# Each of the first nine expert matrices fetched when its own place is free; memory keys turned between value groups; one memory-key tile out of the stretch ahead of the experts

## The chip, the core and the metric

The kernel runs on one core of one Trainium2 chip, as one launch. The metric is device time in microseconds. The engines named below are TensorE (PE, with its weight loads PEld), VectorE (DVE), ScalarE (ACT), GpSimd (POOL) and SyncE (SP), which here only starts transfers. All transfers, whoever starts them, run on the core's 16 DMA engines.

## The reference, cut to what matters

One inference step of two layers over 288 tokens of width 1024 (a prompt of 256, and 8 samples of 4), all in float32. Layer 0 mixes tokens by block-sparse attention and a convolution, layer 1 by a chunked spatial gate; then each layer does this:

```python
for l in range(DEPTH):                       # DEPTH = 2
    ...                                      # mixer; out projection; layer norm 3l
    mk, mv = mem_kv(mem_prompt, w_xkv[l])    # 256 memory rows x 2048 columns: keys, values
    mk_p.append(mk); mv_p.append(mv)         # both are outputs too
    xp = layer_norm(ALPHA * xp + cross_attn(xp, mk, mv, w_xq[l], w_xo[l]), ln_g[l, 1], ln_b[l, 1])
    xs = layer_norm(ALPHA * xs + cross_attn(xs, cache_mem_k[l], cache_mem_v[l], w_xq[l], w_xo[l]), ...)
    xp = layer_norm(ALPHA * xp + moe(xp, w_router, router_bias, w_exp_gate[l], w_exp_up[l], w_exp_down[l]), ...)
    xs = layer_norm(ALPHA * xs + moe(xs, ...), ...)
```

`moe` gives each token to 2 of 16 experts. An expert has three float32 matrices of 2 MB each (gate, up, down), so a layer's experts are 48 matrices, 101 MB.

## The kernel before, in words

**Features lie on partitions** in `feats` (`xT`, `zT`, `mixT`, `qT`, each 128 x 8 x 288). Everything that PE sums in the dense stages goes to four PSUM banks `acc` in turn; `tile_order()` (L144) lists every such tile in order with the engine that empties it, and a tile waits for the one four places ahead of it. PE, DVE and ACT run programs written by hand, in order, joined by semaphores.

**Weights** pass through `ring`, six slots of 2 MB. `unit_order()` (L104) is the list of what is loaded into them; unit u goes to slot u % 6 once the unit six places ahead of it has been read (`slot_free`, L576; `READER` names the tile whose sum ends the reading). SP walks this list strictly in order (`load`, L604), so one unit that isn't free yet holds all behind it. `("xkv", l, n)` is a quarter of layer l's memory projection: n = 0, 1 are the key columns, 2, 3 the value columns. PE makes four key tiles `mk` (`memory_keys`, L910; 2 tiles per unit, 16 matmuls of 256 columns each) and four value tiles `mv` (`memory_values`, L926; 8 matmuls of 512 columns each). Layer 1's memory projection doesn't depend on its tokens, so its tiles are spread as filler: `mk` 0 behind the variance of layer 0's second norm, `mk` 1 behind the `xtok` transposes (L1138) and ahead of the `rank` tile (L1147 and below), `mk` 2, 3 and `mv` 0, 1 behind layer 0's last expert, `mv` 2, 3 around layer 1's `vvar`.

**The experts** run as 16 steps in three sets of three matrices (`place`, L560). Sets 0 and 1 are the six ring slots, set 2 is `EXTRA`: two 16 KB-per-partition pieces of `arena` and one of `feats` (over `mixT` and `qT`). The first three steps are experts 0, 1, 2 whatever the routing, so that their nine matrices can be fetched early (L665 to L671). Steps 3 to 15 are in an order that DVE works out from the router (`steps_ready`); step n's three matrices are fetched when step n-3 is done (`expert_used`). A step is one or more chunks of up to 32 tokens: `gate_and_up` (psS), `pick`, `turn_h`, `down` (psV). POOL stores each chunk's rows to `by_slot`, gathers them behind the last step, and the layer's norm follows.

**Cross attention** (`cross`, L948): `values(0)` and `values(1)` (L1001) sum the cached value rows for two groups of four samples; then `mixT` is projected by `xo`, `mean_tile` and `var` tiles make the norm. The key rows of the prompt's memory are turned back (`mktok`, four tiles of four transposes, L1066) to be stored with the value rows by POOL (`out_mem`), between the mean and the variance of this norm.

The only order that matters around the change is the one written out: PE's program, SP's program and the two lists.

Of the kernel before, what the change touches and what calls it, by code (L numbers as in the profile page):

```python
# [14 lines left out]
P = 128  # L15
# [5 lines left out]
DEPTH = 2  # L21
# [82 lines left out]
def unit_order():  # L104
# [5 lines left out]
    for l in range(DEPTH):  # L110
        if l:
            u += [("in_odd", n) for n in range(4)]
# [15 lines left out]
def tile_order():  # L128
# [49 lines left out]
    for l in range(DEPTH):  # L178
        if l:
            add("u", 8, "s")  # L180
            add("vv", 8, "s")
            add("vmean", 1, "v")
            t.append((f"mv{l}", 2, "s"))
            add("vvar", 1, "v")
            t.append((f"mv{l}", 3, "s"))
# [6 lines left out]
        if l == 0:  # L192
            t.append((f"mv{l}", 2, "s"))
# [17 lines left out]
        add(f"xpvt{l}0", 2, "v")  # L211
        add(f"xspt{l}1", 1, "v")
# [3 lines left out]
        add(f"mktok{l}", 4, "vvss")  # L216
# [7 lines left out]
        if l + 1 < DEPTH:  # L224
            t.append((f"mk{l + 1}", 1, "s"))
        add(f"rank{l}", 1, "v")
        if l + 1 < DEPTH:
            t += [(f"mk{l + 1}", n, "s") for n in (2, 3)] + [(f"mv{l + 1}", n, "s") for n in (0, 1)]
            add(f"xf{l}", 8, "vs")
# [8 lines left out]
def build(nc, x_prompt, x_sample, cache_k, cache_v, state_conv, cache_mem_k, cache_mem_v, page_table,  # L238
# [17 lines left out]
    with ExitStack() as ctx:  # L256
# [308 lines left out]
        for l in range(DEPTH):  # L565
# [3 lines left out]
            for n in range(2):  # L569
# [4 lines left out]
                READER["xkv", l, 2 + n] = (f"mv{l}", 2 * n + 1)  # L574

# [19 lines left out]
        def _(sp):  # L595
# [7 lines left out]
            def load(u, dst8):  # L603
# [19 lines left out]
                if kind[0] == "memV":  # L623
# [5 lines left out]
                    return  # L629
                if kind[0] == "in_even":  # L630
# [10 lines left out]
            while u < len(units):  # L641
# [15 lines left out]
                def expert(e, p, n):  # L657

                    for j in range(3):
                        where, landed, _ = place(l, p, j)  # L660
                        w = (w_exp_gate, w_exp_up, w_exp_down)[j]
                        sp.dma_start(where.rearrange("p (k n) -> p k n", k=(8, 8, 4)[j]),  # L662
                                     w[l, bass.ds(e, 1)].rearrange("a (k p) n -> p (a k) n", p=P)).then_inc(landed, 16)
# [13 lines left out]
                with sp.Fori(1, NE // SETS) as n:  # L677
                    for p in range(SETS):
                        e = expert_at(bass.ds(SETS * n + p, 1))
                        sp.wait_ge(expert_used, NE * l + 1 + p + SETS * (n - 1))  # L680
                        expert(e, p, n)
                e = expert_at(slice(NE - 1, NE))
                sp.wait_ge(expert_used, NE * l + NE - SETS)
                expert(e, 0, NE // SETS)
# [4 lines left out]
        def _(pe):  # L689
# [222 lines left out]
            def memory_keys(l, tiles=range(4)):  # L912
# [3 lines left out]
                for i in tiles:  # L916
                    u = UIDX["xkv", l, i // 2]
# [3 lines left out]
                    for c in range(2):  # L921
                        j = 2 * (i % 2) + c
# [30 lines left out]
            def cross(l):  # L953
# [3 lines left out]
                if l == 0:  # L957
# [1242 lines left out]
```

## Time and profile before

| | |
|---|---|
| median of 3 runs | 1412.68 us (1405.28 to 1412.99) |
| the profiled execution | 1414.48 us, span 1412.8 us |
| PE busy | 1184.6 us (84% of the span) |
| DVE, ACT, POOL busy | 410.6, 264.9, 233.4 us |
| DMA | 360.34 MB, mean 255 GB/s |
| chain that ended last | PE 67%, DVE 9%, DMA 9%, SP's queue 7%, issue 4%, ACT 3% |
| TensorE clock granted, mean | 0.923 of full speed |

The two expert stages stand at 504 to 755 us (layer 0) and 1117 to 1363 us (layer 1). The chain that ended last is the work followed back from the last instruction, at each step to what released it. "SPq" is SP's queue of DMA issues; "issue" is time in which an engine waited for nothing that the profile shows, which covers a wait that PE took in its instruction stream for a transfer that had landed just before.

### The profile page before, as it was taken

The numbers are of one execution on the slowest core, as the hardware profiler recorded it, in microseconds if no ns is written. First come the engines' busy times: TensorE is split into PE (matmuls) and PEld (weight loads), VectorE is DVE, ScalarE is ACT, GpSimd is POOL, SyncE is SP. The second block draws the span as 40 slices with busy tenths as digits, with TensorE's granted clock in tenths as the row PEclk, the third lists the DMA queues.
The fourth block names the chain that finished last, engine by engine and source line by source line (L and its number), as shares of the span: only waits on it lengthen the run. The fifth ranks groups of instructions, "written<-read, shape, count | busy, mean of one in ns | idle before, by whom it ended". The sixth has DMA issues, their size and how long they took to land.

```text
span 1412.8 us, 27325 instructions
## 1 busy us (share of the span) xinstructions
PE 1184.6 (84%) x10800; PEld 790.2 (56%) x10801; DVE 410.6 (29%) x1141; ACT 264.9 (19%) x544; POOL 233.4 (17%) x405
## 2 busy tenths in 40 slices
PE   6998788999979969998758899989988799999640
PEld 4676555577747835554425576768746455555320
DVE  0025546412422432221111302331413522222115
ACT  0004631202310311111101212011302111111011
POOL 2005991000000012222112100000000012222122
PEclk9999989999999879999989899799999799999875
DMA  9646779733563299999999500833565698999941
GB/s 328 230 141 208 238 255 375 284 134 119 212 230 125 87 396 397 341 398 397 399 398 392 195 0 1 300 119 115 189 233 203 255 397 316 398 397 398 397 163 40
DMA packets 158914, 360.34 MB, mean 255 GB/s; under 512 B 9607, under 2 KB 9623, under 8 KB 158842
## 3 DMA queue, kind: packets, MB, share of 16 engines
q1 hardware_dynamic: 145954, 331.50, 63.8%
q0 software_dynamic: 12752, 27.69, 5.5%
q8 instruction: 43, 0.70, 0.2%
q10 hardware_dynamic: 144, 0.27, 0.1%
q14 instruction: 21, 0.17, 0.0%
HBM read 341.47 MB, written 18.38 MB: 255 GB/s over the span
## 4 chain that ended last, share of the span: by engine, by line
PE 67%; DVE 9%; DMA 9%; SPq 7%; issue 4%; ACT 3%; POOL 0%; POOLq 0%; DVEq 0%; ACTq 0%
PE acc L691 37%; PE psS L691 12%; SPq L662 6%; PE psV L691 6%; PE psN L691 5%; DMA feats<-in_w_exp_down 3%; DMA ring<-in_w_exp_down 3%; DVE feats L1388 2%; PE acc L985 2%; PE acc L794 1%; PE psN L1088 1%; DMA ring<-in_w_in_even 1%; ACT feats L2007 1%; DMA arena<-by_slot,arena 1%; PE acc L1138 1%
## 5 line engine op out<-in xcount | busy, mean ns | idle before, releaser
L691 PE MATMUL acc<-feats,ring 128*128 128x288 f32 x1280 | 323.6, 417 | 10.8 <-ACT feats L1924 4.2
L691 PEld LDWEIGHTS acc<-feats,ring 128*128 128x128 f32 x1280 | 249.6, 196 | 83.4 <-issue 9.8
L2130 POOL DMA_DIRECT2D by_slot<-feats x208 | 103.3, 497 | 474.9 <-DVE feats L1765 236.0
L691 PE MATMUL psS<-ring,feats 128*32 128x256 f32 x2176 | 137.5, 409 | 47.9 <-issue 47.9
L691 PEld LDWEIGHTS psS<-ring,feats 128*32 128x32 f32 x2176 | 74.6, 118 | 100.4 <-issue 63.6
L691 PE MATMUL psS<-arena,feats 128*32 128x256 f32 x1408 | 91.1, 409 | 31.4 <-issue 30.9
L1757 DVE TENSOR_TENSOR feats<-feats,psS 64x256 f32<-64x256 f32 x52 | 22.1, 425 | 269.3 <-ACT feats L2017 269.3
L691 PE MATMUL psN<-arena,feats 128*32 128x256 f32 (+1 forms) x1360 | 83.5, 379 | 13.0 <-DVE feats L1723 13.0
L1264 ACT ACTIVATE arena<-acc 128x1024 f32<-128x1024 f32 (+7 forms) x98 | 72.2, 757 | 109.7 <-PE acc L691 34.5
L2017 ACT ACTIVATE feats<-psS 64x256 f32<-64x256 f32 x52 | 19.5, 375 | 358.3 <-PE psS L691 358.3
L691 PEld LDWEIGHTS psS<-arena,feats 128*32 128x32 f32 x1408 | 46.4, 118 | 66.1 <-issue 42.7
L691 PEld LDWEIGHTS psN<-arena,feats 128*32 128x32 f32 x1360 | 44.1, 112 | 41.5 <-issue 14.8
L691 PE MATMUL psV<-ring,feats 128*32 128x256 f32 x1088 | 65.8, 382 | 0.0
L691 PE MATMUL acc<-arena,ring 128*128 128x256 f32 x256 | 58.5, 390 | 0.8 <-ACT arena L1264 0.8
L691 PE MATMUL acc<-ring,arena 128*128 128x512 f32 x128 | 56.7, 597 | 0.0
L1388 DVE SCALAR_TENSOR_TENSOR feats<-arena,cparT,feats 128x256 f32<-128x256 f32 (+1 forms) x180 | 56.4, 388 | 0.0
L691 PEld LDWEIGHTS acc<-arena,ring 128*128 128x128 f32 x256 | 50.0, 197 | 8.4 <-issue 1.2
L1537 DVE SCALAR_TENSOR_TENSOR feats<-feats,acc 128x288 f32<-128x288 f32 x32 | 14.5, 454 | 118.2 <-PE acc L691 118.2
L1765 DVE COPY feats<-psV 128x256 f32 (+1 forms) x52 | 22.1, 425 | 83.1 <-PE psV L691 50.7
L691 PEld LDWEIGHTS psV<-ring,feats 128*32 128x32 f32 x1088 | 31.9, 109 | 23.2 <-DVE feats L1759 5.7
L691 PE MATMUL acc<-arena 128*128 128x256 f32 (+6 forms) x174 | 37.1, 375 | 8.6 <-DVE arena L1354 6.0
L2117 POOL DMA_DIRECT2D out<-arena x2 | 1.5, 730 | 257.4 <-ACT arena L1264 257.4
(336 smaller groups left out, 1297.3 us busy)
## 6 DMA issues: line engine op xcount, KB each, us to landing
ring<-in_w_exp_gate SPq DMA_DIRECT2D x22, 2048.0 KB, 16.9
ring<-in_w_exp_up SPq DMA_DIRECT2D x22, 2048.0 KB, 22.1
ring<-in_w_exp_down SPq DMA_DIRECT2D x22, 2048.0 KB, 19.7
arena<-in_w_exp_gate SPq DMA_DIRECT2D x10, 2048.0 KB, 18.2
arena<-in_w_exp_up SPq DMA_DIRECT2D x10, 2048.0 KB, 22.7
feats<-in_w_exp_down SPq DMA_DIRECT2D x10, 2048.0 KB, 20.0
ring<-in_cache_k SPq DMA_DIRECT2D x64, 256.0 KB, 3.0
ring<-in_cache_v SPq DMA_DIRECT2D x64, 256.0 KB, 3.0
```

The source lines that it names most:

```text
L662: sp.dma_start(where.rearrange("p (k n) -> p k n", k=(8, 8, 4)[j]), w[l, bass.ds(e, 1)].rearrange("a (k p) n -> p (a k) n", p=P)).then_inc ...
L691: return pe.matmul(out, lhsT, rhs, start=first, stop=last)
L794: last = pe.transpose(ACC("kt", 4 * i + b4)[:, 256 * f + P * t:256 * f + P * t + P], K[:, 2 * b4 + t, at:at + P], ident)
L985: last = pe.transpose(ACC(f"xkt{l}", 4 * i + b4)[:, 256 * f + P * t:256 * f + P * t + P], K[:, b4, t, at:at + P], ident)
L1088: last = pe.transpose(psN[:, P * j:P * j + P], XR[:, P * j:P * j + P], ident)
L1264: return lambda out, in_: eng.activation(out, in_, ACT.Copy)
L1388: ins = dve.scalar_tensor_tensor(out=y, in0=u, scalar=tap, in1=y, op0=ALU.mult, op1=ALU.add)
L1537: dve.scalar_tensor_tensor(out=zT[:, i, :], in0=xT[:, i, :], scalar=ALPHA, in1=ACC(stage, i)[:, 0:NTOK], op0=ALU.mult, op1=ALU.add).then_i ...
L1757: dve.tensor_tensor(H[64:128, :], SG[64:128, :], psS[64:128, 0, 0:256], ALU.mult).then_inc(S.h, 1)
L1765: dve.tensor_copy(to, psV[:, 0:256]).then_inc(S.y, 1)
L2017: act.activation(SG[64:128, :], psS[0:64, 0, 0:256], ACT.Silu).then_inc(S.silu, 1)
L2130: pool.dma_start(by_slot[rows, 256 * q:256 * q + 256], YS[32 * q:32 * q + 32, at]).then_inc(S.stored, 16)
```

## The change

- **SP, ahead of the experts.** Before, experts 0 and 1 were fetched as a whole once all three slots of each were free, and expert 2 once the `var` tile and the memory stores were done. Now each matrix has its own wait: the first four ring slots in turn, then `arena`'s first piece behind `xpvt` of group 1, the slot of `xo`'s second half, `arena`'s second piece behind the memory stores, and `feats` behind `var`; expert 1's `down` matrix goes last in layer 0 and ahead of `var` in layer 1.
- **Layer 1's first key unit in halves.** `("xkvh", 1, 0)` and `("xkvh", 1, 1)` are 1 MB each, one key tile each. The slot of the first is free after `mk` 0 alone.
- **`mk` 1 moves** from ahead of `rank` to behind layer 0's last expert; to keep that stretch as long, `mv` 1 moves on to where `mv` 2 was, `mv` 2 to where `mv` 3 was, and `mv` 3 to between the mean and the variance of layer 1's first norm. The unit `("xkv", 1, 3)` is loaded behind the four `in_odd` units.
- **`mktok` moves**, in both layers, from behind the mean of the second norm to between `values(0)` and `values(1)`; the two memory stores can start there.

```diff
@@ unit_order
         if l:
-            u += [("in_odd", n) for n in range(4)]
+            u += [("in_odd", n) for n in range(4)] + [("xkv", l, 3)]
...
-            u += [("xkv", l + 1, 0)]
+            u += [("xkvh", l + 1, 0)]
         u += [("moe", l, n) for n in range(SLOTS)]
         if l + 1 < DEPTH:
-            u += [("pass", l, n) for n in range(3)] + [("xkv", l + 1, n) for n in range(1, 4)]
+            u += [("pass", l, n) for n in range(3)] + [("xkvh", l + 1, 1), ("xkv", l + 1, 1), ("xkv", l + 1, 2)]
@@ tile_order
         add(f"xpvt{l}0", 2, "v")
+        add(f"mktok{l}", 4, "vvss")
         add(f"xspt{l}1", 1, "v")
         add(f"xpvt{l}1", 2, "v")
         add(f"xo{l}", 8, "v")
         add(f"mean{3 * l + 1}", 1, "v")
-        add(f"mktok{l}", 4, "vvss")
@@ SP
+                READER["xkvh", l, n] = (f"mk{l}", n)
...
-                for p in range(2):
-                    for j in range(3):
-                        slot_free(sp, u + 3 * p + j)
-                    expert(p, p, 0)
+                for n in range(4):
+                    slot_free(sp, u + n)
+                    matrix(n // 3, n // 3, n % 3)
+                full(sp, f"xpvt{l}1", 1)
+                matrix(2, 2, 0)
+                slot_free(sp, u + 4)
+                matrix(1, 1, 1)
+                sp.wait_ge(out_mem, 32 * (l + 1))
+                matrix(2, 2, 1)
+                if l + 1 == DEPTH:
+                    slot_free(sp, u + 5)
+                    matrix(1, 1, 2)
                 full(sp, f"var{3 * l + 1}", 0)
-                sp.wait_ge(out_mem, 32 * (l + 1))
-                expert(2, 2, 0)
+                matrix(2, 2, 2)
+                if l + 1 < DEPTH:
+                    slot_free(sp, u + 5)
+                    matrix(1, 1, 2)
@@ PE, norm 3l
-                if l == 0:
-                    memory_values(l, (2,))
+                memory_values(l, (2 + l,))
                 mean_tile(f"var{3 * l}", ...)
@@ PE, cross attention
                 values(0)
+                memory_key_rows()
                 values(1)
...
-                for i in range(4):
-                    ...                      # the mktok transposes
@@ PE, experts
-                if l + 1 < DEPTH:
-                    memory_keys(l + 1, (1,))
                 pe.wait_ge(ones_ready, l + 1)
...
-                    memory_keys(l + 1, (2, 3))
-                    memory_values(l + 1, (0, 1))
+                    memory_keys(l + 1, (1, 2, 3))
+                    memory_values(l + 1, (0,))
@@ PE, layer 1's mixer
+                    memory_values(l, (1,))
+                    mean_tile("vvar", ...)
                     memory_values(l, (2,))
-                    mean_tile("vvar", ...)
-                    memory_values(l, (3,))
```

DVE's and ACT's programs move their share of the same tiles (`cm["mktok"](l)` ahead of `mem_softmax(1)`; `memory_keys` and `memory_values` on ACT with the new numbers).

What stands on PE in layer 0 between the value groups and the first pick of an expert's rows. Here `xspt` are the 2 transposes at L1005 (L1022 after), `xpvt` the 8 at L1021 (L1038), `mktok` the 16 at L1066 (L1069), `memT` the 16 at L909 (L926). Before:

```order
L1021 MATMUL acc<-cst,arena 128x128 x8
L1005 MATMUL acc<-cst,arena 128x128 x2
...
L691 MATMUL acc<-feats,ones_d 128x288 x8
L1066 MATMUL acc<-cst,arena 128x128 x16
L909 MATMUL acc<-cst,arena 128x128 x16
L691 MATMUL acc<-feats,ones_d 128x288 x8
L691 MATMUL acc<-arena,ring 128x256 x16
...
L1138 MATMUL acc<-cst,feats 32x128 x8
L691 MATMUL acc<-arena,ring 128x256 x16
L691 MATMUL acc<-arena 128x16 x3
```

And after:

```order
L1038 MATMUL acc<-cst,arena 128x128 x8
L1069 MATMUL acc<-cst,arena 128x128 x16
L1022 MATMUL acc<-cst,arena 128x128 x2
...
L708 MATMUL acc<-feats,ones_d 128x288 x8
L926 MATMUL acc<-cst,arena 128x128 x16
L708 MATMUL acc<-feats,ones_d 128x288 x8
L708 MATMUL acc<-arena,ring 128x256 x16
...
L1159 MATMUL acc<-cst,feats 32x128 x8
L708 MATMUL acc<-arena 128x16 x3
```

The 16 `mktok` transposes left the place behind the mean (`ones_d`, the first) for the one ahead of group 1's `xspt`, and the 16 matmuls of `mk` 1 between the `xtok` transposes (L1138) and `rank` (128x16) are gone.

On SP, layer 0, from the last `xo` unit to the first fetch by the routed order; `arena` and `feats` are the third set. Before:

```order
L638 DMA ring<-in_w_xkv 128x8x512
L662 DMA ring<-in_w_exp_gate 128x8x512
L662 DMA ring<-in_w_exp_up 128x8x512
L662 DMA ring<-in_w_exp_down 128x4x1024
L662 DMA ring<-in_w_exp_gate 128x8x512
L662 DMA ring<-in_w_exp_up 128x8x512
L662 DMA ring<-in_w_exp_down 128x4x1024
L662 DMA arena<-in_w_exp_gate 128x8x512
L662 DMA arena<-in_w_exp_up 128x8x512
L662 DMA feats<-in_w_exp_down 128x4x1024
```

And after:

```order
L630 DMA ring<-in_w_xkv 128x8x256
L664 DMA ring<-in_w_exp_gate 128x8x512
L664 DMA ring<-in_w_exp_up 128x8x512
L664 DMA ring<-in_w_exp_down 128x4x1024
L664 DMA ring<-in_w_exp_gate 128x8x512
L664 DMA arena<-in_w_exp_gate 128x8x512
L664 DMA ring<-in_w_exp_up 128x8x512
L664 DMA arena<-in_w_exp_up 128x8x512
L664 DMA feats<-in_w_exp_down 128x4x1024
L664 DMA ring<-in_w_exp_down 128x4x1024
```

The same nine matrices and one memory unit, the unit now 1 MB, and experts 1 and 2 interleaved by when their places come free.

On PE, layer 1, from the last half of the `o` projection through the first norm to the query projection. Before:

```order
L691 MATMUL acc<-feats,ring 128x288 x64
L691 MATMUL acc<-feats,ones_d 128x288 x16
L691 MATMUL acc<-feats,ring 128x288 x64
```

And after:

```order
L708 MATMUL acc<-feats,ring 128x288 x64
L708 MATMUL acc<-feats,ones_d 128x288 x8
L708 MATMUL acc<-ring,arena 128x512 x8
L708 MATMUL acc<-feats,ones_d 128x288 x8
L708 MATMUL acc<-feats,ring 128x288 x64
```

The 8 matmuls of `mv` 3 (128x512) now stand between the mean's 8 and the variance's 8.

## Rows read from the trace of the kernel before

**Rows 1.** Timeline of SP's issues: start us, us, what, count.
```profile
490.15 0.37 SPq L662 DMA_DIRECT2D ring<-in_w_exp_gate  x1
...
1127.13 0.38 SPq L662 DMA_DIRECT2D ring<-in_w_exp_gate  x1
```

**Rows 2.** Chain that ended last, in order of time: start us, us, what.
```profile
483.04 7.04 PE acc L691 x32
...
505.38 20.98 DMA feats<-in_w_exp_down
...
1331.10 20.69 DMA ring<-in_w_exp_down
```

**Rows 3.** Timeline of PE, layer 0's experts: [idle before, releaser].
```profile
504.26 5.00 PE L691 MATMUL psS<-ring,feats 128*32 128x256 f32 x64 [1.81 <-issue]
...
754.93 14.08 PE L691 MATMUL acc<-arena,ring 128*128 128x256 f32 x64
768.85 13.90 PE L691 MATMUL acc<-ring,arena 128*128 128x512 f32 x32
```

**Rows 4.** Timeline of PE, layer 1's experts: first step, last step, end.
```profile
1117.43 5.35 PE L691 MATMUL psS<-ring,feats 128*32 128x256 f32 x64 [1.84 <-issue]
...
1353.46 5.35 PE L691 MATMUL psS<-ring,feats 128*32 128x256 f32 x64 [5.33 <-issue]
...
1362.72 0.20 PE L691 MATMUL acc<-cst 128*32 128x1 f32 x2
```

**Rows 5.** Waits, 504 to 755 us: who waited for whom, us, times, longest.
```profile
ACT feats L2017 <- PE psS L691: 184.3, 25, 14.8
...
PE psS L691 <- issue: 47.7, 16, 7.5
```

**Rows 6.** Waits, 1117 to 1363 us.
```profile
ACT feats L2017 <- PE psS L691: 174.0, 27, 14.0
...
PE psS L691 <- issue: 31.2, 16, 6.0
```

**Rows 7.** Windows: us, busy of PE, PEld, DVE, ACT, POOL, clock, DMA share, GB/s.
```profile
1127.00:1352.00 225.00, 193.92 (x3128) 109.61 (x3128) 48.10 (x176) 28.55 (x75) 51.46 (x104) 0.97 1.00 379
546.00:577.00 31.00, 29.90 (x498) 17.02 (x498) 7.32 (x28) 4.57 (x12) 7.94 (x16) 1.00 0.94 357
618.00:647.00 29.00, 22.70 (x376) 13.04 (x376) 6.16 (x22) 3.42 (x9) 7.95 (x16) 1.00 1.04 398
```

**Rows 8.** Timeline of PE, layer 0, value groups to `rank`.
```profile
403.02 1.06 PE L691 MATMUL psV<-ring,arena 128*32 128x512 f32 x8 [0.52 <-DVE arena L1609]
...
410.87 0.41 PE L1005 MATMUL acc<-cst,arena 128*128 128x128 f32 x2 [2.30 <-DVE arena L1608]
411.80 1.93 PE L691 MATMUL psV<-ring,arena 128*32 128x512 f32 x8 [0.52 <-DVE arena L1609]
...
450.77 4.04 PE L691 MATMUL acc<-feats,ones_d 128*128 128x288 f32 x16
454.65 1.47 PE L1066 MATMUL acc<-cst,arena 128*128 128x128 f32 x12
...
461.70 4.53 PE L691 MATMUL acc<-feats,ones_d 128*128 128x288 f32 x16
```

**Rows 9.** Timeline of DVE, layer 0: `mktok` copies, expert mask, wait for `rank`.
```profile
457.59 1.28 DVE L1320 COPY arena<-acc 128x512 f32<-128x512 f32 x2
...
482.09 0.21 DVE L1681 TENSOR_TENSOR arena<-arena,cst 128x48 f32<-128x48 f32 x1
492.02 0.29 DVE L1685 TENSOR_TENSOR arena<-acc,cst 128x128 f32<-128x128 f32 x1 [9.72 <-PE acc L691]
```

**Rows 10.** Timeline of PE, layer 1: first norm's mean and variance, then the query projection.
```profile
934.60 4.04 PE L691 MATMUL acc<-feats,ones_d 128*128 128x288 f32 x16
940.37 4.12 PE L691 MATMUL acc<-feats,ones_d 128*128 128x288 f32 x16 [1.72 <-ACT feats L1918]
948.71 33.98 PE L691 MATMUL acc<-feats,ring 128*128 128x288 f32 x128 [4.22 <-ACT feats L1924]
```

More of the change, by code:

```diff
@@ L182, in tile_order @@
             add("vmean", 1, "v")
+            t.append((f"mv{l}", 1, "s"))
+            add("vvar", 1, "v")
             t.append((f"mv{l}", 2, "s"))
-            add("vvar", 1, "v")
-            t.append((f"mv{l}", 3, "s"))
             add("wm", 2, "v")
@@ L916, in memory_keys @@
                 for i in tiles:
-                    u = UIDX["xkv", l, i // 2]
+                    half = l > 0 and i < 2
+                    u = UIDX["xkvh", l, i] if half else UIDX["xkv", l, i // 2]
                     W = slot(u).rearrange("p (k n) -> p k n", k=8)
@@ L921, in memory_keys @@
                     for c in range(2):
-                        j = 2 * (i % 2) + c
+                        j = c if half else 2 * (i % 2) + c
                         for k in range(8):
@@ L1043, in prompt_values, with memory_key_rows @@
                         last.then_inc(acc_full, 1)
+                def memory_key_rows():
+                    for i in range(4):
+                        t, n = i // 2, i % 2
+                        bank_free(pe, f"mktok{l}", i)
+                        for f in range(4):
+                            evacuated(pe, f"mk{l}", (4 * n + f) // 2)
+                            last = pe.transpose(ACC(f"mktok{l}", i)[:, P * f:P * f + P],
+                                                mkT[l][:, 4 * n + f, P * t:P * t + P], ident)
+                        last.then_inc(acc_full, 1)
                 turn_keys(0)
@@ L1060, in cross @@
                 mean_tile(f"mean{nth}", zT, ones_d[:, :], 8, lambda k: evacuated(pe, f"xo{l}", k))
-                for i in range(4):
-                    t, n = i // 2, i % 2
-                    bank_free(pe, f"mktok{l}", i)
-                    for f in range(4):
-                        evacuated(pe, f"mk{l}", (4 * n + f) // 2)
-                        last = pe.transpose(ACC(f"mktok{l}", i)[:, P * f:P * f + P],
-                                            mkT[l][:, 4 * n + f, P * t:P * t + P], ident)
-                    last.then_inc(acc_full, 1)
                 if l + 1 < DEPTH:
@@ L1630, in _ @@
                 mem_rows(0)
+                cm["mktok"](l)
                 mem_softmax(1)
@@ L1635, in _ @@
                 center(f"mean{3 * l + 1}", zT, 8, centered, 2)
-                cm["mktok"](l)
                 if l + 1 < DEPTH:
@@ L1984, in _ @@
                 mem_rows(0)
+                cm["mktok"](l)
                 mem_softmax(1)
@@ L1987, in _ @@
                 squares(3 * l + 1)
-                cm["mktok"](l)
                 if l + 1 < DEPTH:
@@ L2031, in _ @@
                     act.activation(SD[0:r, t:t + 1], VE[0:r, t:t + 1], ACT.Sqrt).then_inc(sd_ready, 1)
-                    if l + 1 < DEPTH and t == 0:
+                    if l + 1 < DEPTH and t == 1:
                         memory_keys(l + 1, (3,))
```

45 lines of the change are left out of this document (23 added, 22 removed).

## The prediction, made before the changed kernel ran

> **What bounds the kernel now.** I read four views, in this order. The chain that ended last, to see what releases what around the experts; the timeline of SP's issues, to see when each expert matrix could be asked for; PE's timeline and its waits in both expert stages; and the windows, for the DMA rate.
>
> The chain runs through PE for most of the span. In layer 0 it goes through `mk` 1, the 7.04 us from 483.04, and then leaves PE for SP: the fetch of expert 1 waits until that tile has been read, because its `down` matrix uses the slot of layer 1's first key unit. SP holds everything behind it, so experts 1 and 2 are asked for only from 490.15 [rows 1, 2]. The last matrix of expert 2 is issued at 505.38 and lands 20.98 us later, at 526.36, long after the experts began at 504.26 [rows 2, 3]. From there layer 0's stage follows the stream of matrices: PE waits 47.7 us in it, for no engine, which is how a wait for landed weights shows here [rows 5]. The stage lasts from 504.26 to 754.93, 250.7 us, for 25 chunks (the times that ACT takes up a psS) [rows 3, 5].
>
> Layer 1 has no memory tile ahead of its experts. Its stage lasts from 1117.43 to 1362.92, 245.5 us, for 27 chunks, with 31.2 us of such waits [rows 4, 6]. It is the model for what layer 0 becomes, so its rows carry the largest judgement below: step 3's matrices were asked for 9.7 us after the start, at 1127.13; the last one was issued at 1331.10 and landed at 1351.79; the last step began at 1353.46 and took 9.5 us [rows 1, 2, 4].
>
> **The change, part by part.** The sum is made against the profiled execution, 1414.48 us (span 1412.8), which lies 1.8 us above the median of 1412.68.
>
> *`mk` 1 out of the front.* The 16 matmuls of 7.04 us go from between the `xtok` transposes and `rank` [rows 2]. Who is next to be late? DVE's mask, which `rank` needs, is done at 482.30, before 483.04, and DVE then waits 9.72 us for `rank` [rows 9]. So all of it is on the path: **-7.0 us**, at least -6 if DVE or an empty bank takes a little of it.
>
> *The work that replaces it behind the experts* is as long as before: two key and two value tiles took 14.08 and 13.90 us [rows 3]; three and one take 21.1 and 6.95, together 28.1 against 28.0. The key weights come in the order used, 1 MB first, and the stores, gathers and norm behind the last step don't change. **0.** Without the cover of that gather a tile would cost 7 us.
>
> *The nine matrices.* What is gained is not six matrices' worth. At 398 GB/s [rows 7] a matrix of 2.097 MB takes 5.27 us, so six landed ahead are 31.6 us of stream. But the stream can't go on into step 3 before step 0 has been computed: it ran from 14.1 us before the start (490.15 against 504.26) and will go on only 9.7 us after it, as layer 1's did. Of 31.6 us, 23.8 are lost in that pause, and 7.8 are left; more of the early slots then are still in use when SP gets to them, as in the window of the four-chunk step, where the rate is 357 [rows 7]. The better estimate is layer 1 itself: 245.5 us for 27 chunks. Two chunks fewer store 0.26 MB less (a chunk's 32 rows are 0.131 MB), 0.7 us of a stream that sets the end. So layer 0's stage takes 244.8 instead of 250.7: **-5.9 us**; -8 if no more slots hold it than before, -3 if its own order of long steps idles the stream more than layer 1's.
>
> *`mktok` between the value groups, in each layer.* DVE copies two of the tiles, 1.28 us [rows 9], ahead of group 1's softmax, for which PE already waits 2.30 us [rows 8]. That adds 1.3 us. The 16 transposes are about 2.0 us (12 took 1.47) and lie in that wait, now 3.6 us long. Behind the mean they are gone, and the variance can start about 1.9 us earlier: it can't at once, since in layer 1's first norm, with nothing between, it starts 5.8 us after the mean does, and in layer 0's second 10.9 us after it with `mktok` and `memT` between [rows 8, 10]. There is a second effect: group 1's psV matmuls take 1.93 us where group 0's took 1.06 [rows 8], at two such places, since PE had idled; with the gap filled up to 1.7 us come back. I take half, 0.9. Net per layer +1.3 - 1.9 - 0.9 = -1.5, so **-3.0 us** for both, with bounds of +1 and -6.
>
> On that clock the Trainium skill says that the slow state is the default and that activity of the array lifts it ("TensorE: Matmul & The Clock Gate", What's actually happening). By it the filled gap would give back all 1.7 us in each layer and the sum would be 1.6 us lower; by the rows alone it may be nothing. No row here has transposes filling that gap.
>
> *`mv` 3 between mean and variance of layer 1's first norm.* A value tile is 6.95 us (13.90 for two [rows 3]). PE idles only 1.72 us there before the variance [rows 10]; the 4.22 us of idle behind the variance can't be used, since the tile stands ahead. So **+5.2 us**, at worst +7 (if the idle time comes back elsewhere). The tiles at `vmean` and `vvar` have the same size as those that stood there: 0. The unit of `mv` 3 now holds its slot until this norm, and SP holds the cached keys of three slots behind it; three such units are 16 us at 5.27 us each, and the query projection alone is 34 us [rows 10], so they still come first.
>
> *The stores and single waits.* The 2 MB of memory rows go out beside the loads of the `xo` stage instead of an idle stretch; nobody waits for either there but SP's own later fetches, which have until the experts begin. 0.
>
> Sum: -7.0 - 5.9 - 3.0 + 5.2 = -10.7. The profiled execution would be 1403.8, the median **1402.0 us**.
>
> **The rivals.**
>
> *The stalls vanish* (the nine matrices give a lead that lasts). Then layer 0's 47.7 us of waiting would shrink to some 16 ordinary step changes of about 1 us: -31.7 instead of -5.9, 1376 us. Against it stands layer 1, which started with such a lead and waited 31.2 us all the same, with 5.33 us still before its last step [rows 4, 6]. 4 in 100.
>
> *Everything a bit better*: -8 for the stage, all of the clock given back, variance 2.5 us earlier, and the norm's idle time leaving the clock up so that the query projection loses less. About -16 to -18, 1396 us. 14 in 100.
>
> *The tile costs in full and `mktok` gives nothing*: -7 - 5.9 + 7 + 1 = -5, down to -3: 1408 us. For it speaks that PE's waits there hang on DVE and ACT, whose work is not less. 12 in 100.
>
> *Slower: the restarted stream runs slower.* Layer 0's end is set by the bytes behind the pause: 39 matrices and some 24 chunks of stores, 84.9 MB. At layer 1's mean of 379 GB/s [rows 7] they take 224 us; at 357, the rate of layer 0's own worst stretch, 238, which is 13.8 us more and turns the sum into +3.1, 1416 us. It decides from a mean of 362 GB/s on. Against it: the 398 in full stretches of both layers. 6 in 100.
>
> The Trainium skill speaks for that rival: it gives about 358 GB/s as what one core gets from HBM ("DMA: Bandwidth & Descriptors", Specifications). By it the 84.9 MB would take 237 us and the kernel 1415. The trace doesn't agree: 379 over 225 us, and 398 where no slot is missing [rows 7].
>
> **How the numbers follow.** The forecast (from -7 to -14 us) has 64 in 100; it is by far the likeliest. About 1% is what a measurement of this kernel can tell from no change, 14 us here; -10.7 is 0.76%. Faster by more: the stalls vanish (4), most of "a bit better" (13), and the upper end of the forecast (8): 0.25. Slower by over 1% needs a stream under 345 GB/s or two costs missed: 0.04. The rest, 0.71, is within 1%. The range leaves out the vanishing stalls below and the slower stream above, and takes in most of the other two: 1395 to 1410.
>
> **What would show each step.** In the profile of the changed kernel: no 16 matmuls of 128x256 between L1159 and `rank`, and DVE's wait for `rank` near 2.7 us instead of 9.72. The last of the nine matrices landed some 15 us before the first psS. A first expert step about 8.5 us earlier, near 496; step 3's fetch some 9.7 us behind it; a stage of 244 to 246 us, with its waits for weights mostly in the last eight steps, as in layer 1. In the value groups a DVE wait of PE near 3.6 us less 2.0 of transposes. In layer 1's first norm no idle time between `mv` 3 and the variance, and the variance 11 us after the mean's start instead of 5.8. Layer 1's stage as long as before, 245.5 us. The prediction is wrong if layer 0's stage isn't 242 to 248 us, or if the key loads of layer 1 come late.

## The result and the profile after

The changed kernel took **1391.44 us** (median of 5 runs, 1386.82 to 1394.18) beside 1410.17 us for the kernel before (5 runs, 1405.28 to 1412.99): a ratio of **0.9879** with an interval of 0.9851 to 0.9907. So it is faster by 1.2%, or 18.7 us, where 10.7 were forecast, and it lies 3.6 us below the low end of the range. The forecast started from 1412.68 us, the median of three runs; the median of five is 2.5 us lower, and that is part of the miss. The profiled execution took 1394.18 us with a span of 1392.5 us; that of before had 1412.8.

| | before | after |
|---|---|---|
| span of the profiled execution | 1412.8 us | 1392.5 us |
| PE busy | 1184.6 us | 1170.4 us |
| chain: PE, DVE, DMA, SP's queue, issue | 67, 9, 9, 7, 4% | 68, 9, 8, 6, 4% |
| TensorE clock granted, mean | 0.923 | 0.929 |

PE is busy 14.2 us less, though the change takes no instruction away from it. No step of the forecast beyond 1.8 us of clock shortens busy time, so most of the surprise must lie there.

SP's issues of layer 0 in the kernel after (start us, us, what, count), which answer to [rows 1]:

```profile
404.03 0.37 SPq L664 DMA_DIRECT2D ring<-in_w_exp_gate  x1
...
432.58 0.37 SPq L664 DMA_DIRECT2D ring<-in_w_exp_gate  x1
...
469.23 0.37 SPq L664 DMA_DIRECT2D ring<-in_w_exp_down  x1
502.99 0.39 SPq L664 DMA_DIRECT2D ring<-in_w_exp_gate  x1
```

Expert 1 is asked for from 432.58 instead of 490.15, the last of the nine at 469.23, and step 3's matrices at 502.99, 10.6 us behind the first psS.

PE of the kernel after, from the value groups to the end of layer 0's experts (start us, us, what, idle before and its releaser), which answer to [rows 3, 8]:

```profile
405.71 1.91 PE L1069 MATMUL acc<-cst,arena 128*128 128x128 f32 x16
409.55 0.41 PE L1022 MATMUL acc<-cst,arena 128*128 128x128 f32 x2 [1.93 <-DVE arena L1627]
410.48 1.06 PE L708 MATMUL psV<-ring,arena 128*32 128x512 f32 x8 [0.52 <-DVE arena L1628]
...
447.91 4.04 PE L708 MATMUL acc<-feats,ones_d 128*128 128x288 f32 x16
...
456.56 5.74 PE L708 MATMUL acc<-feats,ones_d 128*128 128x288 f32 x16
...
477.95 0.81 PE L708 MATMUL acc<-arena 128*128 128x16 f32 x6 [0.23 <-issue]
...
738.03 20.99 PE L708 MATMUL acc<-arena,ring 128*128 128x256 f32 x96
```

And DVE where it reads `rank`, which answers to [rows 9]:

```profile
480.14 0.29 DVE L1704 TENSOR_TENSOR arena<-acc,cst 128x128 f32<-128x128 f32 x1 [2.29 <-PE acc L708]
```

The 16 `mktok` transposes lie in what was a wait, group 1's psV takes 1.06 us where it took 1.93, and DVE waits 2.29 us for `rank` instead of 9.72.

The rest of the account is made by stages: the same milestones (the first instruction of a named tile) in two profiles of each kernel, the one above and one of the same code taken with the experiments. Microseconds, before first:

| stage | before | after | moved | forecast |
|---|---|---|---|---|
| L0 value groups to `xtok` (`mktok`, layer 0) | 74.64, 75.24 | 72.89, 72.90 | -2.0 | -1.5 |
| L0 `xtok` to DVE's read of `rank` (`mk` 1 gone) | 14.36, 13.65 | 6.92, 6.93 | -7.1 | -7.0 |
| L0 experts, first psS to end | 250.74, 252.75 | 245.73, 245.56 | -6.1 | -5.9 |
| end of experts to layer 1's `u` projection | 40.33, 40.56 | 43.16, 42.81 | +2.5 | 0 |
| L1 `u` and `v` projections | 64.76, 65.00 | 63.73, 63.89 | -1.1 | 0 |
| L1 mix and `o` projection | 47.30, 45.62 | 40.09, 40.09 | **-6.4** | 0 |
| L1 first norm (`mv` 3) and query projection | 54.84, 53.82 | 58.67, 58.73 | +4.4 | +5.2 |
| L1 value groups to router (`mktok`, layer 1) | 64.58, 63.83 | 61.79, 61.70 | -2.5 | -1.5 |
| L1 experts | 245.50, 245.58 | 246.41, 246.54 | +0.9 | 0 |

The rows of this table give -17.4. The stretch ahead of all of it, where both kernels have the same instructions, differs by 0.6 between the means (it ends at 403.02 and 398.47 us before, 400.33 and 399.87 after), and the rest moves by 0.2 or less; that makes, rounding aside, the 17.8 us between the means of the two spans.

### The profile page after: what moved, and what is told of

Its sections match the earlier page's. It is cut to its first block, busy times and chain, and to the rows that moved or that the text cites. A ratio compares the mean times of both kernels' runs of the same rounds, so it can differ in the third digit from the quotient of the medians.

```text
span 1392.5 us, 27311 instructions
## 1 busy us (share of the span) xinstructions
PE 1170.4 (84%) x10800; PEld 779.9 (56%) x10801; DVE 410.0 (29%) x1141; ACT 264.8 (19%) x544; POOL 233.5 (17%) x405
## 4 chain that ended last, share of the span: by engine, by line
PE 68%; DVE 9%; DMA 8%; SPq 6%; issue 4%; ACT 4%; POOL 0%; POOLq 0%; DVEq 0%; ACTq 0%
PE acc L708 37%; PE psS L708 13%; PE psV L708 6%; SPq L664 5%; PE psN L708 5%; DMA ring<-in_w_exp_down 3%; DVE feats L1407 2%; PE acc L1002 2%; DMA feats<-in_w_exp_down 1%; PE psN L1109 1%; PE acc L811 1%; DMA arena<-by_slot,arena 1%; ACT feats L2023 1%; DMA ring<-in_w_in_even 1%; ACT arena L1283 1%
## 5 line engine op out<-in xcount | busy, mean ns | idle before, releaser
L708 PE MATMUL acc<-feats,ring 128*128 128x288 f32 x1280 | 317.4, 411 | 11.2 <-ACT feats L1943 4.2
L708 PEld LDWEIGHTS acc<-feats,ring 128*128 128x128 f32 x1280 | 245.8, 193 | 81.4 <-issue 10.1
L708 PEld LDWEIGHTS acc<-ring,arena 128*128 128x128 f32 x128 | 24.8, 193 | 28.2 <-issue 27.3
L1937 ACT ACTIVATE feats<-feats 128x576 f32<-128x576 f32 x16 | 10.7, 683 | 156.9 <-DVE feats L1537 156.9
```

Of the source, the lines that this page charges most:

```text
L708: return pe.matmul(out, lhsT, rhs, start=first, stop=last)
```

## The experiments

**The same kernels again**, to see how far medians and stages repeat (no edit).

> The kernel before, unchanged, for a second profile of it. Two theories of why the change gave some 18 us where 10.7 were forecast. Clock by chance: in the one profile of before the TensorE clock had fallen to its lower level from about 889 to 905 us (mix matmuls 12.2 us, out projection 34.2) and in the one after it had not (7.8 and 31.3), though the same instructions stand there; if it is chance, this profile may show either, and the median should lie at 1405 to 1413, ratio 1.00. Clock by cause: if the change itself keeps the clock up there, this profile shows the low clock again, mix 12.2 us.

> The changed kernel, unchanged, for a second profile and a median on the same chip as the three that follow: 1389 to 1393, ratio 0.986 to 0.989. In all four profiles so far with layer 0's experts ending earlier, the mix matmuls of layer 1 took 7.8 us and the output projection 31.3 us at full clock; if that belongs to the changed kernel and isn't chance of one run, it shows again.

`before_again` gave 1408.22 us, a ratio of 0.9981 (0.9959 to 1.0002) to before; `after_again` 1393.5 us, 0.9868 (0.9831 to 0.9906). The second profiles are the second numbers of the table. Its stages agree within 0.4 us in the kernel after and within 2 us in the kernel before; a single profile can't carry a term of 1 us there. The stretch ahead of the value groups repeats worse: over all fourteen profiles of this study the same instructions end between 394.6 (`undo_mktok`) and 403.0 us, so a whole span can't be read as the effect of an edit. The mix with its `o` projection is shorter in both profiles of the kernel after (40.09 us each) than in either of the kernel before (47.30 and 45.62).

**The fetches undone.** The changed kernel with SP's waits of before: experts 0 and 1 as a whole, then expert 2.

```diff
-                for n in range(4):
-                    slot_free(sp, u + n)
-                    matrix(n // 3, n // 3, n % 3)
...
+                for p in range(2):
+                    for j in range(3):
+                        slot_free(sp, u + 3 * p + j)
+                    expert(p, p)
```

> The changed kernel with the old waits of SP ahead of the experts: experts 0, 1 and 2 each as a whole. mk 1 stays behind the experts, so expert 1 can be asked for at about 469 us, behind mk 0, and expert 2 right behind it, where before it was 490. My theory: the lead matters only up to the start of the experts plus step 0; six matrices from 469 are landed by about 503, step 2 starts at 512, so almost nothing is lost: 0 to 2 us slower than the changed kernel, 1391 to 1394. Rival: the single waits carry the gain of the stage; then 5 us slower, 1396.

It took 1395.17 us, 0.9881 (0.9854 to 0.9908). Its layer-0 experts last 246.28 us, though SP asks for expert 1 only at 468.79, as its issues show:

```profile
468.79 0.37 SPq L664 DMA_DIRECT2D ring<-in_w_exp_gate  x1
...
484.00 5.33 SPq L664 DMA_DIRECT2D feats<-in_w_exp_down  x1
504.00 0.39 SPq L664 DMA_DIRECT2D ring<-in_w_exp_gate  x1
```

So with `mk` 1 out of the way the old waits bring the stage to within 0.6 us of its new length. The slot that comes free after `mk` 0 alone does the work; the nine single waits, the part with which the title begins, add what can't be told from nothing: of the kernels measured beside `undo_fetch`, those with the single waits had medians of 1391.4 and 1391.7 us, but each has another edit too.

**The keys back in front.** The other half: single waits and the `mktok` move, but memory units, `mk` 1 and all value tiles as before.

```diff
-            u += [("xkvh", l + 1, 0)]
+            u += [("xkv", l + 1, 0)]
...
+                if l + 1 < DEPTH:
+                    memory_keys(l + 1, (1,))
                 pe.wait_ge(ones_ready, l + 1)
```

> The changed kernel without the part on mk 1: layer 1's first key unit whole, mk 1 between the xtok transposes and rank, the value tiles as before; the single fetches and the moved mktok stay. My step: the tile is 7.0 us of path in front and mv 3 gives 4.9 back, so the first expert starts 7 us later than in the changed kernel and the first norm of layer 1 is 4.9 us shorter; with the stage at 246 us all the same (nine matrices landed before it). Where the clock falls in the mix again (E to u as in before), 6 us more; where not, 2 us slower than the changed kernel. So 1393 to 1401. Rival: the stage is shorter by what the stream gains in 7 us, then no slower than the changed kernel.

It took 1395.9 us, 0.9895 (0.9855 to 0.9934), over runs from 1388.56 to 1406.97. `rank` is late again, as DVE's timeline shows, and the stage short all the same (245.82 us):

```profile
483.79 0.29 DVE L1703 TENSOR_TENSOR arena<-acc,cst 128x128 f32<-128x128 f32 x1 [8.73 <-PE acc L705]
```

Here eight of the nine matrices were asked for by 459.53, and the ninth at 481.87. This profile is the fastest of its six runs. Either edit alone therefore shortens layer 0's experts, and both together no more than one. And moving `mk` 1 with all the tiles that followed it is nearly a zero-sum trade: by the stages it saves 6.4 us ahead of `rank` (13.37 against 6.92), and costs 4.9 in the first norm and 2.6 behind layer 0's experts. The medians, 1395.9 beside 1391.4 and 1393.5, would give it a gain of 2 to 5 us, which their intervals don't tell from nothing.

**The `mktok` move undone.**

```diff
                 values(0)
-                memory_key_rows()
                 values(1)
...
                 mean_tile(f"mean{nth}", zT, ones_d[:, :], 8, lambda k: evacuated(pe, f"xo{l}", k))
+                memory_key_rows()
```

> The changed kernel with the turned memory keys back behind the mean of the second norm in both layers (and the first piece of arena fetched only when they have been read). My theory from the trace after: the move gives 0.2 and 1.0 us at the value groups and about 1 to 2 us at the variance in each layer, so this is 3 to 5 us slower than the changed kernel, 1395. Rival: it gives nothing outside clock chance, 1391.

SP's fetch of `arena`'s first piece waits here for the last `mktok` tile and comes behind expert 1's `up` matrix. 1391.72 us, 0.9866 (0.9842 to 0.9891): no difference in the median. The profile has the stages of before again in both layers (in layer 0, 7.86 us from the first psV to group 1's `xspt` and 41.21 from there to the mean, where the kernel after has 9.22 and 38.36; in layer 1, 15.93 us from the second norm's mean to the router where it has 14.11), which adds up to some 4 us lost, and layer 1's experts 1.9 us shorter. The stretch ahead of the value groups, which the edit doesn't touch, is 5.5 us shorter, which is why the span (1389.7 us) shows no loss. What the move is worth by the stages, 4.5 us, and what the medians allow, about 3 at most, don't meet; I leave that open.

**The value tiles back.** `mv` 0, 1 behind the experts, `mv` 2, 3 around `vvar`, nothing between the first norm's mean and variance.

```diff
-                memory_values(l, (2 + l,))
+                if l == 0:
+                    memory_values(l, (2,))
                 mean_tile(f"var{3 * l}", ...)
...
-                    memory_values(l + 1, (0,))
+                    memory_values(l + 1, (0, 1))
```

> The changed kernel with the four value tiles where they stood before (0 and 1 behind layer 0's last expert, 2 and 3 at layer 1's vvar), so nothing between the mean and variance of layer 1's first norm. If the tile there costs its 4.9 us and the fill behind the experts (now 35 us) still ends before the last normed row (37 us behind the last expert in the changed kernel), this is 4 to 5 us faster than the changed kernel: about 1386 to 1387. If the fill then sets the end of that stretch, the gain is 0 to 2 us.

1391.37 us, 0.9869 (0.9840 to 0.9897), the same median as the changed kernel. In its profile the first norm has its 14.11 us again (-4.9), the stretch behind layer 0's experts 41.6 us (-1.4) and layer 1's experts 242.9 (-3.5), while the `u` and `v` projections, the `o` projection and layer 1's value groups together take 3.6 us more, at a lower clock. The span is 1386.8 us, 5.7 below the changed kernel's; the medians show none of it.

**The mix and the clock.** The stage that nobody had forecast holds the same instructions in both kernels and the same idle time ahead of it. PE of the kernel before there:

```profile
887.30 12.20 PE L691 MATMUL acc<-arena 128*128 128x128 f32 x48 [1.09 <-ACT arena L1264]
900.61 34.15 PE L691 MATMUL acc<-feats,ring 128*128 128x288 f32 x128 [1.11 <-DVE feats L1573]
```

And its windows there (us, busy of PE, PEld, DVE, ACT, POOL, clock, DMA share, GB/s):

```profile
887.00:892.00 5.00, 4.70 (x22) 3.91 (x22) 2.85 (x9) 0.00 (x0) 0.51 (x1) 0.73 1.05 393
892.00:900.00 8.00, 7.51 (x27) 6.20 (x26) 4.38 (x14) 0.00 (x0) 0.00 (x0) 0.50 1.05 388
```

PE of the kernel after:

```profile
872.20 7.84 PE L708 MATMUL acc<-arena 128*128 128x128 f32 x48 [1.09 <-ACT arena L1283]
881.14 31.31 PE L708 MATMUL acc<-feats,ring 128*128 128x288 f32 x128 [1.11 <-DVE feats L1592]
```

And its window:

```profile
872.00:880.00 8.00, 7.80 (x48) 6.51 (x48) 6.41 (x21) 0.00 (x0) 0.51 (x1) 1.00 1.05 389
```

The 48 matmuls take 12.20 us with the clock granted at 0.50, the lower of its two levels (1.2 GHz), from about 2 us after their start, and 7.84 us at 1.00 (2.4 GHz). Ahead of the fall PE had done 24 short transposes, idled 1.09 us and begun the mix, in both kernels. The theory: what decides is where this light stretch falls against the moments at which the clock may change, and the change shifted it by luck. It says that a few useless matmuls ahead of it can make the kernel before faster and the kernel after slower. The rival, that some edit is the cause (less memory projection at `vvar`, a quieter DMA), says that they only add their own time. The added matmuls write a bank that the tile behind them overwrites.

```diff
@@ pad_before (the kernel before); in pad_after (the kernel after): i == 2, range(5)
                     bank_free(pe, f"mv{l}", i)
+                    if l == 1 and i == 3:
+                        for _ in range(3):
+                            mm(ACC(f"mv{l}", i)[:, 0:256], memT[l][:, 0, P * t:P * t + P], W[:, 0, 0:256], True, True)
```

> The kernel before with work added: three extra matmuls of 256 columns (about 1.3 us, overwritten, no effect on the output) ahead of mv 3 in layer 1's mixer, some 7 us before the mix matmuls. Theory A, position: the clock falls there only because the short idle behind the vtok transposes lies badly against the clock's own steps (it fell about 2.0 us after the mix began in both profiles of before; in the four others a step of the clock would lie 1.0 to 1.7 us behind that start). Then 1.3 us of extra work moves it out, mix takes 7.8 instead of 12.2 us, and the kernel gets faster by 3 to 5 us: 1404 to 1406 on the same chip where before has 1409. Theory B, cause elsewhere (what was loaded or run earlier in the change): 1.3 us slower, mix still 12.2.

> The changed kernel with five such extra matmuls (about 2.2 us) ahead of mv 2, which stands at the same place. Theory A, position: this moves the mix to where it stands in before against the clock's steps; the clock falls, mix takes about 12 us and the output projection 33 to 34: 2.2 + 4.3 + 2 = 8 us slower than the changed kernel, about 1399. Theory B: 2.2 us slower, 1393.

Before with 1.3 us of work added took 1403.76 us beside 1408.05: 0.9959 (0.9932 to 0.9986), **faster by 4.3 us** between the medians. After with 2.2 us added took 1400.54 us, 0.9924 (0.9892 to 0.9957), which is 7.0 us above `after_again` in the same session. PE of the two, `pad_before` first:

```profile
865.44 8.32 PE L691 MATMUL acc<-ring,arena 128*128 128x256 f32 x22
...
879.35 7.84 PE L691 MATMUL acc<-arena 128*128 128x128 f32 x48 [1.12 <-ACT arena L1267]
888.30 31.31 PE L691 MATMUL acc<-feats,ring 128*128 128x288 f32 x128 [1.11 <-DVE feats L1576]
```

```profile
856.96 9.19 PE L708 MATMUL acc<-ring,arena 128*128 128x256 f32 x26
...
871.69 12.15 PE L708 MATMUL acc<-arena 128*128 128x128 f32 x48 [1.09 <-ACT arena L1286]
884.96 34.20 PE L708 MATMUL acc<-feats,ring 128*128 128x288 f32 x128 [1.11 <-DVE feats L1595]
```

The two lengths have changed places, 7.84 against 12.15 us, and the medians went with them in both directions. The rival falls: the kernel before keeps the clock without any of the edits, and the kernel after loses it with all of them. For `pad_before` the median says so too; for `pad_after` the medians alone would hardly tell 7.0 us from the 2.2 of added work, and the row of the mix decides. That moments at which the clock may change exist by themselves is not shown by any row; that 1.3 or 2.2 us of shift decide is. The profile of `pad_before` is one of its two fastest of twelve runs, whose mean granted clock goes from 0.926 to 0.934, so some of the others may have lost the clock there. An estimate from the two rows: (12.20 - 7.84) + (34.15 - 31.31) = 7.2 us for one such fall; `before_again`, where the clock came back sooner, lost 5.5.

**The gather ahead of the loads.** Behind layer 0's experts the norm waits for its gathered rows, and the stage table charged 2.5 us there to a stretch that I had called unchanged. The theory: the 2 MB loads for layer 1, which SP starts as soon as slots are free, share the 16 DMA engines with the last stores and the gather. The test holds them until the gather has landed, in the kernel after and in the kernel before.

```diff
+                if units[u] == ("in_odd", 0):
+                    sp.wait_ge(gathered[2], 32)
                 if units[u][0] != "moe":
                     slot_free(sp, u)
```

> The changed kernel with SP holding the four in_odd loads until layer 0's rows have been gathered. In the changed kernel DVE's first gathered row tile came 20.1 us behind the last expert, in before 18.3, and in layer 1, where nothing is loaded beside it, 12.5. Theory: the in_odd and xkv loads share the DMA engines with the stores and the gather. If so the first tile comes 3 to 6 us earlier (14 to 17), the u projection starts 3 to 5 us earlier, and the kernel gains 3 to 5 us unless the fill of 28 us on PE or a late in_odd takes it. Rival: what is slow is the gather itself (POOL's issue and small rows), then nothing changes at the gather and in_odd may come late: 0 to 3 us slower.

> The kernel before with SP holding the in_odd loads until layer 0's rows are gathered. If the loads beside it are what delays the gather, the first gathered tile comes about 5.6 us earlier (12.7 instead of 18.3 behind the last expert, as in gather_first), and the u projection starts about 7 us earlier (33 instead of 40.3 behind it, the fill of 28 us then sets it): 1401 to 1404, less or more 6 us by whether the clock falls in the mix. Rival: the gather was slowed only in the changed kernel; then no change.

After with the hold took 1387.38 us, 0.9827 (0.9797 to 0.9857), 6.1 us below `after_again`; before with it 1398.91 us, 0.9888 (0.9846 to 0.9931). The gather, in the order before, after, `gather_first`, is DVE's wait for `by_slot`, one row or two from its timeline:

```profile
773.25 1.28 DVE L1783 SCALAR_TENSOR_TENSOR arena<-arena 128x1024 f32<-128x1024 f32 x1 [17.50 <-DMA arena<-by_slot,arena]
```

```profile
758.18 1.28 DVE L1802 SCALAR_TENSOR_TENSOR arena<-arena 128x1024 f32<-128x1024 f32 x1 [19.33 <-DMA arena<-by_slot,arena]
...
763.45 1.28 DVE L1802 SCALAR_TENSOR_TENSOR arena<-arena 128x1024 f32<-128x1024 f32 x1 [0.91 <-DMA arena<-by_slot,arena]
```

```profile
751.29 1.28 DVE L1804 SCALAR_TENSOR_TENSOR arena<-arena 128x1024 f32<-128x1024 f32 x1 [11.91 <-DMA arena<-by_slot,arena]
```

It waits 11.91 us where nothing loads beside it, as it does in layer 1, where nothing is left to load (from the experts' end it is 12.5 us there, and 12.7 in this one), 17.50 in the kernel before and 19.33 in the kernel after, which also asks for its four `in_odd` units within 10.1 us instead of 16.6. Part of it is POOL's wait for its last stores to land, ahead of the gather; the kernel after, then `gather_first`:

```profile
746.79 0.18 POOL L2155 TENSOR_TENSOR arena<-arena 1x1 f32<-1x1 f32 x1 [4.54 <-DMA by_slot<-feats]
```

```profile
744.07 0.18 POOL L2157 TENSOR_TENSOR arena<-arena 1x1 f32<-1x1 f32 x1 [1.28 <-DMA by_slot<-feats]
```

The stores give 3.3 of the 7.4 us, the gather itself the rest. The stretch from the experts' end to `u` falls from 43.0 to 32.9 us, and in `before_gather` from 40.4 to 33.2: with the loads held both kernels have the same length there, so the 2.5 us of the stage table are the loads' doing. The median of `gather_first` follows by 6. This profile, the slowest of its six runs, has the mix at the low clock (11.78 us), which may be where part of the rest went. The median of `before_gather` lies 14.6 us below the kernel before in its session, twice what its stretch explains; its `u` and `v` projections are 2.7 us shorter, with the clock at full speed through both, and what the rest is stays open.

On this the Trainium skill says that transfers started by different engines run on the same 16 DMA engines and interleave ("DMA: Bandwidth & Descriptors", Issuing engines are not separate DMA queues). The trace agrees as far as it goes: DVE waits 7.4 us longer for POOL's stores and gather with SP's loads beside them.

**The value tile behind the variance, and both moves.** In `values_behind_var` the tile `mv` 3 stands behind layer 1's first variance, where PE idled 4.22 us for the query projection [rows 10]; `both_moves` has the hold of the loads too.

```diff
-                memory_values(l, (2 + l,))
+                if l == 0:
+                    memory_values(l, (2,))
                 mean_tile(f"var{3 * l}", ...)
+                memory_values(l, (3,))
```

> The changed kernel with mv 3 behind the variance of layer 1's first norm instead of ahead of it. Ahead it cost 4.9 us since only 1.7 us of idle was there; behind it PE idles 4.2 us for the normalised rows. So 6.95 - 4.2 = 2.7 us instead of 4.9, and the projection behind it may start at full clock (31.3 instead of 32.9 us): 2 to 4 us faster than the changed kernel, 1388 to 1391. Rival: the place makes no difference: 1392.

> values_behind_var together with gather_first. gather_first alone was at 1387 beside 1393 of the changed kernel, with the clock low in the mix. The two places are apart, so the gains should add: 1383 to 1386, ratio about 0.980. If the mix keeps its clock, 1378 to 1380.

`values_behind_var` took 1386.46 us, 0.9824 (0.9786 to 0.9862); `both_moves` **1378.12 us**, 0.9742 (0.9706 to 0.9777), the best version of the study: 35.4 us below the kernel before in its session. PE of `both_moves`:

```profile
861.01 7.84 PE L710 MATMUL acc<-arena 128*128 128x128 f32 x48 [1.09 <-ACT arena L1285]
...
908.56 4.12 PE L710 MATMUL acc<-feats,ones_d 128*128 128x288 f32 x16 [1.72 <-ACT feats L1939]
912.52 7.03 PE L710 MATMUL acc<-ring,arena 128*128 128x512 f32 x16
919.38 21.02 PE L710 MATMUL acc<-feats,ring 128*128 128x288 f32 x86
```

No idle time is left ahead of the query projection. From the first norm's mean to the first turned key rows, 58.7 us in the kernel after become 54.5, as in the kernel before without any tile there (54.84 and 53.82) and 0.7 us more than in `values_back` (53.82): behind the variance the tile is nearly free. Both medians lie below what was expected, the second in the range given for a mix that keeps its clock.

Its mix also settles how far the clock's draw is a matter of the kernel. `gather_first` has the same instructions as `both_moves` up to the mix and reached it 0.12 us apart. Windows of `gather_first`, then of `both_moves`:

```profile
861.00:863.00 2.00, 2.00 (x13) 1.68 (x14) 0.92 (x4) 0.00 (x0) 0.51 (x1) 1.00 1.05 387
863.00:865.00 2.00, 2.00 (x10) 1.76 (x9) 1.78 (x7) 0.00 (x0) 0.00 (x0) 0.60 1.05 385
```

```profile
861.00:863.00 2.00, 1.99 (x13) 1.68 (x13) 0.80 (x3) 0.00 (x0) 0.51 (x1) 1.00 1.05 385
863.00:865.00 2.00, 2.00 (x14) 1.68 (x14) 1.93 (x8) 0.00 (x0) 0.00 (x0) 1.00 1.05 387
```

One falls inside the mix; the other stays up through it and falls 9.7 us after its start, in the `o` projection, which then takes 33.00 us. So the same code can draw either. It doesn't look like an even draw: over all other profiles but the two paddings the mix was low in both of the kernel before and in `before_gather`, and high in both of the kernel after and in `undo_fetch`, `undo_mktok`, `values_back`, `keys_in_front` and `values_behind_var`. So few profiles can't give the odds, but a kernel seems to have its own, and a shift of 1 to 2 us ahead of the mix changes them.

## Why the prediction was wrong, step by step

**`mk` 1 out of the front: right.** -7.1 us against -7.0, DVE's wait 2.29 us against "near 2.7".

**The nine matrices: right in size, wrong in what does it.** The stage lasts 245.6 us against 244.8 forecast, taken from layer 1's, and its waits for landed weights are 40.7 us, as the waits of the kernel after say:

```profile
PE psS L708 <- issue: 40.7, 16, 6.8
```

But the forecast put the gain down to the early fetch of all nine. `undo_fetch` and `keys_in_front` have the gain with part of the lead each; beyond that more lead buys nothing. What sets the stage then is its own stream and steps, and the clock: `pad_after` has the same code there and took 242.5 us, with 0.94 granted where the kernel after had 0.91. Layer 1's experts, the model for the forecast, also took 242.9 to 246.5 us over the profiles. So the 0.8 us between forecast and result are in part luck. The argument against "the stalls vanish" holds further than I took it.

**`mktok`: the order of work right, the clock's share luck.** Two terms came as described: +1.4 us at the value groups (+1.3 forecast), and the variance 2.3 us earlier in layer 0 and 1.8 in layer 1 (1.9), while layer 0's `var` tile went from 4.53 to 5.74 us. The third is psV: I took half of the clock's gain, 0.9 us a layer, and in both profiles of the kernel after all of it came back (1.06 and 1.07 us). But the filled gap doesn't hold the clock. With the transposes in the same place psV took 1.77 to 1.94 us again in layer 1 of six other profiles, and 1.93 in layer 0 of one of them (`keys_in_front`); here `values_back`, layer 1:

```profile
1013.08 0.41 PE L1024 MATMUL acc<-cst,arena 128*128 128x128 f32 x2 [1.93 <-DVE arena L1629]
1014.01 1.93 PE L709 MATMUL psV<-ring,arena 128*32 128x512 f32 x8 [0.52 <-DVE arena L1630]
```

The stages give -4.5 instead of -3.0; the medians don't confirm it, and up to 1.5 us a layer of it is such a draw.

**`mv` 3 between mean and variance: right.** 19.01 us from the mean to the query projection where it was 14.11: +4.9 against +5.2. With what the projection gains on the clock behind it, +4.4. The variance starts 10.75 us after the mean (11 forecast).

**The work behind the experts: wrong.** The step said that "the key weights come in the order used" and that stores, gathers and norm don't change. Its instructions don't; the loads beside them do. They cost 2.5 us more than before, and holding them takes 7.3 us off that stretch in the kernel before and 10.1 in the kernel after, which no step of mine had seen.

**The step that failed is one that the sum hasn't got.** It has a term for the clock only where the change fills a gap, in the value groups. Of the tiles at `vmean` and `vvar` it says that they "have the same size as those that stood there: 0". That holds for them (27.2 us from `vmean` to the mix in both kernels), but not for what stands behind them, and the projections and the mix of layer 1 have no term at all. Every edit also shifts what follows, and layer 1's mix and `o` projection lie at the edge of the clock's fall: -6.4 us, most of the 8 us between forecast and result. The paddings show that this is a matter of position, so the change got it by luck. The others (-1.5 for `mktok`, -1.1 in the `u` and `v` projections, -0.8 at `mv` 3, +2.5 behind the experts, +0.9 in layer 1's experts) nearly cancel. The row of the mix, 12.20 us at a clock of 0.50, stood in the trace of the kernel before; nothing in the forecast asked what could move it. The range had no room for it either: it was made from the terms' own bounds, and the rival that came nearest, "everything a bit better" at 1396, got there with other terms.

The chance of a gain over 1% stood at 0.25, and it was one, 0.93 to 1.49% by the interval. Without the mix it would have been near 12 us, 0.9% (an estimate: 18.7 - 6.4).

## What to carry to other kernels

Before costing an edit, look for places where a run of matmuls takes two lengths in two profiles of the same code, or has a granted clock of 0.50 inside a dense stretch; each is a term of several us that any shift ahead of it can draw or lose, and belongs in the range with both signs. A gain of that kind isn't the change's own: add a microsecond of work and see whether it stays. And where the path waits for a small gather or store, ask what large loads start at the same moment; holding them back until it has landed gave 6 us in the median here.

## What the hardware showed that I had not expected

- The granted clock fell 2.0 to 2.5 us after the mix's start in all five profiles in which the mix was slow (before 2.03, `before_again` 2.27, `before_gather` 2.35, `gather_first` 2.49, `pad_after` 2.08), and never inside it in the other nine; in two of these it fell just behind the mix, 8.6 us (`values_back`) and 9.7 us (`both_moves`) after its start. The Trainium skill says that what the gate judges by is free-running and doesn't reset when a kernel starts ("TensorE: Matmul & The Clock Gate", What's actually happening). By that each execution would draw its own outcome. `gather_first` against `both_moves` agrees; the two pairs of repeated profiles, and medians that 1.3 and 2.2 us of padding moved by -4.3 and +7, suggest that the odds differ by kernel.
- POOL's last stores and its gathers took 11.9 us of DVE's time up to the first row used with no loads beside them, and 17.5 to 19.3 us beside four loads of 2 MB.
